# Two transformer blocks on one core: the scan's corner product moved to the decays' bank, masks ahead of weight splitting, the convolution's SiLU and product one block later, and the output sent from two queues

## The reference

```python
# block 1, the gated linear scan of one of 8 heads (chunks of 64)
b = cumsum(log_g)
scores = einsum('bhtk,bhtsk,bhsk->bhts', q, exp(b_t - b_s) below the diagonal, k)
o = scores @ v + (q * exp(b)) @ S          # S: the state from the chunks before
y_a = rms_norm(o) * silu(hg)
# beside it: banded attention of 16 heads, sigmoid gates, projection, FFN relu(u W)^2 W'

# block 2: gMLP branch, neighbourhood attention, gates, projection, and
def conv_ffn(x, g_norm, w_up, conv_k, conv_b, w_down):
    up = rms_norm_2(x, g_norm) @ w_up                 # 2 * 5504 columns
    up = pad[:, :t] * conv_k[0] + pad[:, 1:t + 1] * conv_k[1] + pad[:, 2:t + 2] * conv_k[2] + conv_b
    gate, val = split(up)
    return x + (silu(gate) * val) @ w_down            # 5504 x 2048
return rms_norm_2(x, norm_final)
```

## Time and profile before

| | us |
|---|---|
| median of 3 runs | 2916.78 (2915.05 to 2916.95) |
| the profiled execution | 2916.44 |
| its span, first to last instruction | 2914.7 |
| TensorE busy in it | 2857.6 (98%) |
| DVE busy | 2174.6 (75%) |
| ACT busy | 1506.9 (52%) |

### The profile page before, as it was taken

The page is one execution under the profiler, slowest core; times in us unless marked ns, Lnnn a source line. Parts: engine busy times, 40 slices in busy tenths (PEclk is TensorE's granted clock), DMA queues, the critical chain, the costliest instruction groups (busy, mean ns, idle before and its releaser), DMA issues.

```text
span 2914.7 us, 42894 instructions
## 1 busy us (share of the span) xinstructions
PE 2857.6 (98%) x16334; PEld 2457.6 (84%) x16334; DVE 2174.6 (75%) x3307; ACT 1506.9 (52%) x2256; POOL 131.8 (5%) x121
## 2 busy tenths in 40 slices
PE   8999999999999999999998999999999999999998
PEld 6888888888888888888887888888888888888887
DVE  7777777778767777777786666767867887777776
ACT  5555555556554444444464555556555455555555
POOL 0000000000100000000050000000010000000002
PEclk9999999999999999999999999999999999999999
DMA  6445545445555555555554555555555565555553
GB/s 221 165 158 165 158 157 165 158 148 186 189 185 194 183 195 186 193 185 195 183 194 148 167 182 167 174 183 180 188 174 173 180 203 194 187 185 193 189 187 123
DMA packets 157020, 520.22 MB, mean 178 GB/s; under 512 B 28944, under 2 KB 31376, under 8 KB 156816
## 3 DMA queue, kind: packets, MB, share of 16 engines
q1 hardware_dynamic: 155376, 513.90, 54.2%
q10 hardware_dynamic: 1440, 3.59, 0.3%
HBM read 515.32 MB, written 2.10 MB: 178 GB/s over the span
## 4 chain that ended last, share of the span: by engine, by line
PE 81%; DVE 12%; ACT 3%; issue 2%; DMA 0%; SPq 0%; ACTq 0%; DVEq 0%; POOL 0%; POOLq 0%
PE acc L346 37%; PE acc L351 18%; PE psT L346 7%; PE psX L346 7%; DVE w_lo L1059 4%; PE psT L351 4%; PE psX L351 4%; ACT w_hi L676 2%; PE acc_first L346 1%; DVE HS L1202 1%; PE psS L488 1%; DVE HS L1211 1%; PE psT L480 1%; PE psA L438 0%; DVE work L1065 0%
## 5 line engine op out<-in xcount | busy, mean ns | idle before, releaser
L1059 DVE TENSOR_TENSOR w_lo<-w_raw,w_hi 128x1024 fp32r<-128x1024 f32 (+1 forms) x960 | 1170.1, 1226 | 389.1 <-ACT w_hi L676 364.3
L346 PE MATMUL acc<-XU,w_hi 128*128 128x512 f32 x3472 | 1130.8, 398 | 3.9 <-issue 3.4
L676 ACT ACTIVATE w_hi<-w_raw 128x1024 fp32r<-128x1024 f32 (+1 forms) x960 | 992.1, 1049 | 266.7 <-PE acc L346 159.5
L351 PEld LDWEIGHTS acc<-XU,w_lo 128*128 128x128 f32 x3472 | 653.4, 188 | 150.9
L346 PE MATMUL acc<-XY,w_hi 128*128 128x512 f32 x2112 | 691.6, 400 | 5.1 <-DVE G L1065 4.6
L351 PE MATMUL acc<-XU,w_lo 128*128 128x256 f32 x3472 | 683.8, 278 | 0.0
L346 PEld LDWEIGHTS acc<-XU,w_hi 128*128 128x128 f32 x3472 | 544.4, 189 | 10.5 <-issue 6.7
L351 PEld LDWEIGHTS acc<-XY,w_lo 128*128 128x128 f32 x2112 | 399.0, 189 | 93.4 <-DVE XY L1251 2.4
L351 PE MATMUL acc<-XY,w_lo 128*128 128x256 f32 x2112 | 417.3, 279 | 2.1 <-DVE XY L1251 2.1
L346 PEld LDWEIGHTS acc<-XY,w_hi 128*128 128x128 f32 x2112 | 331.9, 190 | 14.3 <-issue 5.8
L681 ACT ACTIVATE cross<-acc 128x256 f32<-128x256 f32 x297 | 112.5, 379 | 262.7 <-PE acc L346 262.7
(11 more groups left out here) (233 smaller groups left out, 2479.3 us busy)
## 6 DMA issues: line engine op xcount, KB each, us to landing
w_raw<-in_weights SPq DMA_DIRECT2D x956, 512.0 KB, 3.6
bias<-in_rel_bias SPq DMA_DIRECT2D x8, 384.0 KB, 5.8
bias<-in_rpb_back SPq DMA_DIRECT2D x32, 96.0 KB, 6.5
w_raw<-in_weights SPq DMA_DIRECT2D x8, 384.0 KB, 3.1
hT<-in_x_t SPq DMA_DIRECT2D x8, 256.0 KB, 6.5
out_dram<-G ACTq DMA_DIRECT2D x4, 512.0 KB, 3.1
G<-in_range_sums ACTq DMA_DIRECT2D x1, 576.0 KB, 3.5
G<-in_pair_masks ACTq DMA_DIRECT2D x1, 576.0 KB, 4.7
```

The source lines that it names most:

```text
L346: return nc.tensor.matmul(bank[:, :], hi[:, k, col:col + P], X[:, k0 + k, :], start=first and k == 0, stop=last and k == nk - 1 and k % 2 ...
L351: return nc.tensor.matmul(bank[:, 0:T], lo[:, k, col:col + P], X[:, k0 + k, 0:T], start=False, stop=last and k == nk - 1 and k % 2 == 0, s ...
L676: act.activation(w_hi[s][:, 0:n], w_raw[s][:, 0:n], ACT.Copy).then_inc(hi_done, 1)
L1059: V.tensor_tensor(w_lo[s][:, 0:n], w_raw[s][:, 0:n], w_hi[s][:, 0:n].bitcast(F32), ALU.subtract).then_inc(lo_ready, 1)
```

## The change

1. `tile_pairs` (the corner product) writes psE[:, T:T + P] instead of psA[:, 0:P], waits for the fourth `decay_exp` instead of the fourth `psA_read`, and is issued after block 16 instead of 18. ACT copies from there.
2. In DVE's iteration 16 of `heads1`, `low_part` comes after the masks, the addition and `softmax_back`.
3. In ffn2, ACT's SiLU and high copy go to the next iteration, behind its `round_block`; DVE's low half of the product goes to the next iteration, behind its `low_part`.
4. A preload of the table set with Ln and Exp stands ahead of `ffn2last`, and `final_tile` squares before it copies.
5. At the end ACT scales and sends three quarters of rows 128 to 255, DVE scales the last quarter, and SP, the weights' queue, sends it and rows 0 to 127.

```diff
@@ -36,6 +36,7 @@
 LEAD = 4
 RAW = 4
 KB = 8
+OUT_ACT = 3 * D // 8
 BLOCK = KB * P
 
 
@@ -327,7 +328,13 @@
                         if name == "heads1" and i == 0 and b == 1:
                             for q in range(4, 8):
                                 load_x(q)
-            sp.wait_ge(S("out_done"), 16 * 2 * NT)
+            for c in range(2):
+                sp.wait_ge(S("out_scaled0"), c + 1)
+                sp.dma_start(out[0, 0:P, c * D // 2:(c + 1) * D // 2], Gf[:, c * D // 2:(c + 1) * D // 2])\
+                  .then_inc(S("out_done"), 16)
+            sp.wait_ge(S("out_scaled0"), 3)
+            sp.dma_start(out[0, P:2 * P, 2 * OUT_ACT:D], Gf[:, D + 2 * OUT_ACT:2 * D]).then_inc(S("out_done"), 16)
+            sp.wait_ge(S("out_done"), 16 * 5)
 
 
         @block.tensor
@@ -441,8 +448,8 @@
 
             def tile_pairs(i):
 
-                pe.wait_ge(S("psA_read"), i * 4 + 4)
-                nc.tensor.matmul(psA[:, 0:P], kTop[:, :], HS[:, 1, 3, :], start=True, stop=True).then_inc(S("top_full"), 1)
+                pe.wait_ge(S("decay_exp"), i * 4 + 4)
+                nc.tensor.matmul(psE[:, T:T + P], kTop[:, :], HS[:, 1, 3, :], start=True, stop=True).then_inc(S("top_full"), 1)
 
             def scan_out(i):
                 pe.wait_ge(S("AT_ready"), i + 1)
@@ -505,8 +512,7 @@
                 13: [scores(0, P, 1)],
                 14: [pair_products(2), decays(3), transpose_pair(wk(5), "avz_ready", "avT_full", "v_ready")],
                 15: [scores(1, T, 1)],
-                16: [pair_products(3)],
-                18: [tile_pairs],
+                16: [pair_products(3), tile_pairs],
                 19: [scan_out, prob_transposes(0, 1)],
                 20: [attend(0, 1), prob_transposes(1, 1)],
                 21: [scan_rms, attend(1, 1)],
@@ -784,7 +790,7 @@
                         softmax_exp(1, T, 1, i)
                     if b == 18:
                         act.wait_ge(S("top_full"), i + 1)
-                        act.activation(AT[:, 1, :], psA[:, 0:P], ACT.Copy).then_inc(S("top_copied"), 1)
+                        act.activation(AT[:, 1, :], psE[:, T:T + P], ACT.Copy).then_inc(S("top_copied"), 1)
                     if b == 19:
                         act.wait_ge(S("o_full"), i + 1)
                         act.activation(wk(0), psE[:, 0:T], ACT.Copy).then_inc(S("o_copied"), 1)
@@ -926,17 +932,30 @@
 
                 act.wait_ge(acc_free, p.tile(0, j) + 1 + TILE_CREDIT)
                 if j >= 2:
+                    act.wait_ge(S("sqf_added"), j - 1)
+                act.activation(wk(6 + j % 2), hT[:, j, :], ACT.Square).then_inc(S("sqf_ready"), 1)
+                if j >= 2:
                     act.wait_ge(S("outT_full"), j - 1)
                 act.activation(sqb[:, j % 2, :], hT[:, j, :], ACT.Copy,
                                scale=cols[:, C_FIN2 + j:C_FIN2 + j + 1]).then_inc(S("hw_ready"), 1)
-                if j >= 2:
-                    act.wait_ge(S("sqf_added"), j - 1)
-                act.activation(wk(6 + j % 2), hT[:, j, :], ACT.Square).then_inc(S("sqf_ready"), 1)
-
-            def ffn2(name, i):
+
+            def conv_late(u, n):
+
+                if u is None:
+                    return
+                if u.value == 0:
+                    act.wait_ge(S("gate_conv"), n + 1)
+                    act.activation(wk(4), wk(2), ACT.Silu).then_inc(S("gate_silu"), 1)
+                else:
+                    act.wait_ge(S("act2_z"), n + 1)
+                    act.activation(XY[:, ring_half(u.group, u.t), 0:T], wk(5), ACT.Copy).then_inc(S("act2_hi"), 1)
+
+            def ffn2(name, i, late):
                 p, tile, c = ph[name], 0, 0
                 for b, s in enumerate(FFN[name]):
                     round_block(p, i, b)
+                    conv_late(*late)
+                    late = (None, 0)
                     if b and complete(FFN[name][b - 1]):
 
                         u = FFN[name][b - 1]
@@ -945,12 +964,7 @@
                         ch = n + u.value * FF2
                         act.activation(wk(2 + u.value), work[:, u.value, 0:T], ACT.Identity, scale=convc[:, 0, ds(ch, 1)],
                                        bias=convc[:, 3, ds(ch, 1)]).then_inc(S("conv_first"), 1)
-                        if u.value == 0:
-                            act.wait_ge(S("gate_conv"), n + 1)
-                            act.activation(wk(4), wk(2), ACT.Silu).then_inc(S("gate_silu"), 1)
-                        else:
-                            act.wait_ge(S("act2_z"), n + 1)
-                            act.activation(XY[:, ring_half(u.group, u.t), 0:T], wk(5), ACT.Copy).then_inc(S("act2_hi"), 1)
+                        late = (u, n)
                     if complete(s):
                         free_cross(p, i, tile)
                         copy_cross(p, i, c, b, ffn_bank(name, tile))
@@ -958,11 +972,13 @@
                     if name == "ffn2last" and b:
                         final_tile(p, b - 1)
                     tile += s.half if s.kind == "up" else (2 if s.group < 0 else 1)
-
-            ffn2("ffn2first", 0)
+                return late
+
+            late = ffn2("ffn2first", 0, (None, 0))
             for i in range(ph["ffn2"].iters):
-                ffn2("ffn2", i)
-            ffn2("ffn2last", 0)
+                late = ffn2("ffn2", i, late)
+            act.preload_act_table_set("natural_log_exp_and_others")
+            ffn2("ffn2last", 0, late)
             final_tile(ph["ffn2last"], KD - 1)
 
 
@@ -972,14 +988,10 @@
             act.wait_ge(S("out_rstd"), 1)
             act.wait_ge(S("out_copied"), KD)
             for c in range(2):
-                part = Gf[:, D + c * D // 2:D + (c + 1) * D // 2]
+                part = Gf[:, D + c * OUT_ACT:D + (c + 1) * OUT_ACT]
                 act.activation(part, part, ACT.Copy, scale=small[:, 7:8]).then_inc(S("out_scaled1"), 1)
                 act.wait_ge(S("out_scaled1"), c + 1)
-                act.dma_start(out[0, P:2 * P, c * D // 2:(c + 1) * D // 2], part).then_inc(S("out_done"), 16)
-            for c in range(2):
-                act.wait_ge(S("out_scaled0"), c + 1)
-                act.dma_start(out[0, 0:P, c * D // 2:(c + 1) * D // 2], Gf[:, c * D // 2:(c + 1) * D // 2])\
-                   .then_inc(S("out_done"), 16)
+                act.dma_start(out[0, P:2 * P, c * OUT_ACT:(c + 1) * OUT_ACT], part).then_inc(S("out_done"), 16)
 
 
         @block.gpsimd
@@ -1150,7 +1162,7 @@
             p = ph["heads1"]
             for i in range(p.iters):
                 for b in range(p.blocks):
-                    if p.block(i, b):
+                    if p.block(i, b) and b != 16:
                         low_part(p, i, b)
                     t = b // 2
                     bank = acc_first if t == 0 else acc[(t - 1) % 2]
@@ -1231,6 +1243,7 @@
                         softmax_front(1, T, 1, i)
                     if b == 16:
                         softmax_back(1, T, 1, i)
+                        low_part(p, i, b)
                     if b in (17, 19, 21):
                         n = (b - 15) // 2
                         tile_sum(p, i, 7 + n, b, 7 + n, bank, wk(8))
@@ -1416,10 +1429,18 @@
                     link(V.memset(work[:, val, edge:edge + 1], 0.0))
             dve.wait_ge(rs_ready, 4)
 
-            def ffn2(name, i):
+            def low_product(n, at):
+                dve.wait_ge(S("act2_hi"), n + 1)
+                mark(V.tensor_tensor(XY[:, at, T:2 * T], wk(5), XY[:, at, 0:T].bitcast(F32), ALU.subtract),
+                     S("act2_ready"), n + 1)
+
+            def ffn2(name, i, late):
                 p, tile, c = ph[name], 0, 0
                 for b, s in enumerate(FFN[name]):
                     low_part(p, i, b)
+                    if late is not None:
+                        low_product(*late)
+                        late = None
                     if b and complete(FFN[name][b - 1]):
 
                         u = FFN[name][b - 1]
@@ -1435,9 +1456,7 @@
                             link(ins)
                             dve.wait_ge(S("gate_silu"), n + 1)
                             mark(V.tensor_tensor(wk(5), wk(4), y, ALU.mult), S("act2_z"), n + 1)
-                            dve.wait_ge(S("act2_hi"), n + 1)
-                            mark(V.tensor_tensor(XY[:, at, T:2 * T], wk(5), XY[:, at, 0:T].bitcast(F32), ALU.subtract),
-                                 S("act2_ready"), n + 1)
+                            late = (n, at)
                     if complete(s):
                         z = work[:, s.value, 1:T + 1]
                         tile_sum(p, i, c, b, tile, ffn_bank(name, tile), z)
@@ -1450,16 +1469,17 @@
                         if name == "ffn2last" and s.t >= 3:
                             copy_out(s.t - 3)
                     tile += s.half if s.kind == "up" else (2 if s.group < 0 else 1)
+                return late
 
             def copy_out(j):
                 dve.wait_ge(S("outT_full"), j + 1)
```

(8 more changed lines are left out.)

## The result

| | before | changed |
|---|---|---|
| median of 6 runs (lowest to highest), us | 2916.72 (2915.05 to 2916.95) | 2892.72 (2892.14 to 2893.18) |
| changed over before, 95% interval | | 0.9919 [0.9906, 0.9932] |
| profiled execution / its span, us | 2916.44 / 2914.7 | 2892.62 / 2890.8 |
| TensorE's share of the chain that ended last | 81% | 92% |

The change takes 24.0 us off, 0.8%. The prediction was 2895.2, with a range of 2892.5 to 2902.5, so the result lies at the range's lower end, 0.2 us inside it.

What follows compares the result with a forecast made beforehand. TensorE was taken to bound the kernel, so only its waits count (VectorE sets ffn2first's laps). Gains of 13.6, 7.2 and 2.0 less 1.4 made 21.4 us off, forecasting 2895.2 us; range 2892.5 to 2902.5 (8 in 10).

Steps and rivals of the forecast that it cites:

- Corner product and masks: heads1: TensorE's 1.70 us hole before the corner product closes whole in eight iterations, 13.6 us gained; bounds 8.4 to 13.6.
- The change cuts the chain twice: heads1: psE removes the corner product's late wait, and masks and softmax precede `w_lo`; one joint term of 13.6 us.
- Convolution: ffn2first: eight laps shrink from 14.08 to TensorE's 13.25 us once VectorE stops setting them, 7.2 us gained; lower bound 5.3.
- once both waits go: ffn2first: without VectorE's 1.50 us wait for `w_hi` and 0.56 for the high half, its lap is 12.0, under TensorE's 13.25.
- The listed waits: ffn2first: TensorE's eight waits for `w_lo` before a down tile, 5.3 us in all, taken as the gain's lower bound.
- Entry of ffn2last: First down product: low half now follows two adds and `w_lo`, so TensorE starts later; 1.4 us lost once, bounds 0 to 2.0.
- End: Output tail: 1.29 us from the table load, 0.3 from an earlier first send, up to 0.4 from holes; 2.0 together, bounds 1.0 to 3.0.
- SP's filling of ScalarE's holes: Output transfers: splitting sends over two queues can only fill holes in ScalarE's issue, worth 0.4 us at most.
- the two that brought a wait back: Rivals: heads, TensorE waits before block 20, 2901.7 (10%); ffn2first, a new hand-over takes back its 7.2 us, 2902.5 (7%).
- half a hole at block 20: Heads, rival, 10%: VectorE's chain slips 1.2 us, so TensorE waits 0.8 before block 20, eight times, 6.4 us: 2901.7.
- No load came back before Ln or Exp: Tail, rival, 5%: the preload isn't kept or a load returns, losing 1.29 or 2.6 us: 2896.6 to 2898.
- ffn2 has no wait of TensorE: ffn2, slower rival, 3%: late SiLU holds ScalarE's queue over 32 tiles; waits above 3.3 us per lap cost, at 4.2 reaching 2924.

Runs made afterwards that it cites:

- the entry undone: Changed kernel with the last ffn2 tile's high and low halves made at once, as before the change: 2892.07 us, ratio 0.9916.
- both doses: Changed kernel with three, or one, unused 128x256 multiplies added in VectorE's iteration 16 of the heads: 2902.56 us with three, 2894.71 us with one.
- the four edits: Kernel before with only masks first, SiLU late, the table preload and the square ahead of the copy: 2891.75 us, ratio 0.9915.

## Why the prediction was right

**Corner product and masks: 13.6 predicted, 14.9 measured.** The mechanism held: mask multiply as soon as VectorE is free, `w_lo` at its 3.15 us later (3.18 measured, 595.03 to 598.21), block 20's bank 0.36 us ahead. The term was too small by 0.15 an iteration. The prediction had the two short matmuls "still cost the same 0.24 us". In block 16 they cost 0.14 from their start to the next (591.77 to 591.91); before, behind a hole, 0.24. The rest, 0.05, is unassigned. In other words the whole distance in the earlier trace rows should have been the term: 611.87 - 609.69 - 0.23 = 1.95, less the 0.14 or less that the product costs among others: 1.8 and a little over. The stated bound, that above 13.6 nothing is left, was therefore wrong.

**"The change cuts the chain twice": wrong.** It is cut once, by the masks' place. The corner product's bank alone moved the wait to block 20, and the masks alone gave everything. The sum was right, since the prediction took both edits as one term, but by its own walk the mask multiply at 607.6 would have freed the old bank in time too.

**Convolution: 7.2 predicted, 7.4 measured**, with laps of 13.24 for 13.25. The step "once both waits go" asked for more than was needed: either one is enough over eight laps. The listed waits (5.3 us) were the lower bound and missed 2.1 us of it; the lap was the better view.

**Entry of ffn2last: 1.4 predicted, 1.4 measured.** The walk had TensorE 1.37 late of the earlier trace rows; it came 1.28 behind its undisturbed start and lost 0.11 more before its next product. It belongs to the late product alone.

**End: 2.0 predicted, 1.8 measured** (1.4, and 0.4 from the square, counted at nothing). That the two totals are so close is partly luck: the square's gain stands in for the holes' that didn't come. The first output transfer goes out 2.01 us after the first of the last four short sums (2881.38 to 2883.39), before 3.64 (2903.78 to 2907.42): 1.63 sooner, as said. The part for SP's filling of ScalarE's holes, up to 0.4, was not there: from the first send to the span's end it takes 7.45 us, before 7.24, so 0.2 of the 0.33 gained at the first send were given back. On the table load the chip decided between the row's 1.29 and the 2.66 of the Trainium skill (ScalarE: Activation LUTs, What ACT_TABLE_LOAD costs): with the preload alone Exp came 1.28 us sooner after the sums, so the drain is not on this path. The Trainium skill's rule that several issuing engines save only issue time (Trainium Kernel Development and Optimization, Key Constraints) agrees with the trace: the split alone gave 0.1 us at the end of its profile and nothing in the median.

**What was not in the sum.** The terms measured make 14.9 + 7.4 + 1.8 - 1.4 = 22.7. The profiled pair differs by 23.8: the other 1.1 are 1.5 less at branch1's entry, 0.1 less in the stages between and 0.5 more in the start-up. The start-up is the same program in both. At branch1's entry a kernel that is the changed one up to there (the entry undone) had the slower clock, so the 1.5 can't be booked to the change (below); without these the change is worth about 23 us.

**Rivals.** Of the two that brought a wait back, half a hole at block 20 didn't come, but its place was well chosen: it is the one that the added multiplies open. In ffn2first VectorE had 0.99 us of waits left in a lap, none of which TensorE saw. No load came back before Ln or Exp, and ffn2 has no wait of TensorE.

## What to carry to other kernels

When one engine waits inside a chain, first ask which instruction could run in that gap; moving the consumer's buffer only moved the stall two blocks on. Price a removed stall by the distance between the neighbours' starts, or by the lap, rather than by the listed wait, and a new wait by what the lead of the buffers can absorb over the number of laps. Test each part of a bundle alone: of seven edits three gave nothing that can be measured (the corner's bank, the late product beside the late SiLU, the split), and the late product cost 1.4 us at the last phase's entry.

## What the runs showed of the hardware that was not expected

At the entry of branch1 TensorE waits 2.09 us for the low half of XY, in every kernel here. In some profiles its granted clock then falls to half, 1.2 of 2.4 GHz, for some 3 us, and in others it stays whole. Windows of two microseconds behind that wait, first the kernel before, then the changed one; the last figures are granted clock, DMA share and GB/s:

```profile
629.60:631.60 2.00, 2.00 (x7) 1.71 (x8) 1.29 (x2) 1.99 (x4) 0.00 (x0) 0.50 0.03 8
```

```profile
615.16:617.16 2.00, 2.00 (x13) 1.73 (x13) 1.29 (x2) 1.99 (x4) 0.00 (x0) 1.00 0.03 8
```

Seven matmuls run in the one and thirteen in the other, in the same span of time and at the same place in the program; between these two profiles it costs 1.5 us. Whole clock stood in both profiles of the changed kernel and in those of the corner's move alone and the split alone. Half clock stood in the profiles of before, masks alone, SiLU alone, product alone, preload alone, the entry undone, both doses, and the four edits. What decides it is open: the wait ahead of it is as long in all of them, and the changed kernel and the one with the entry undone, which are the same program up to there, stand on different sides.
